# The chunked recurrence of a two-block transformer step: TensorE's twelve steps written as a loop, with one copy of two operands

## The chip, the cores and the metric

The kernel runs on one core of a Trainium2 chip, in float32 with some matmuls in the rounded form fp32r. The metric is the device time of one execution in microseconds (us). Before the change three runs gave 2889.7, 2894.3 and 2896.8 us; the median is 2894.3 us. The profile is of one further execution, whose span is 2891.0 us.

## The reference

The program computes two transformer blocks over 512 latent tokens (the second with 256 context tokens as well). Nearly all of it is left alone by the change. What matters here is one part of the second block, a gated delta rule (RWKV-7), run forward and backward over 768 tokens for 8 heads of 64 dimensions:

```python
def wkv7_scan(state0, r, w, k, v, a_vec, b_vec, reverse):
    xs = tuple(t.transpose(1, 0, 2, 3) for t in (r, w, k, v, a_vec, b_vec))

    def step(S, inp):
        r_t, w_t, k_t, v_t, a_t, b_t = inp
        sa = jnp.einsum('bhij,bhj->bhi', S, a_t)
        S = (S * w_t[:, :, None, :] + sa[..., None] * b_t[:, :, None, :]
             + v_t[..., None] * k_t[:, :, None, :])
        return S, jnp.einsum('bhij,bhj->bhi', S, r_t)

    s_fin, ys = lax.scan(step, state0, xs, reverse=reverse)
    return s_fin, ys.transpose(1, 0, 2, 3)
```

The other parts (projections, two attention mixers, a dense and two sparse feed-forward layers) stand before and after it.

## The kernel before

Each part of the network is a `Stage` with one method for each engine. Semaphores that only count upwards order the engines; `at(name, n, i)` gives the count that item i of step n has when it is done. The stage that changes is `Wkv`, from 1351 to 1672 us of the span. It works through the 768 tokens in `STEPS` = 12 chunks of 64 tokens, with all 8 heads and both directions at once, so that each product is 16 matmuls of 64x64 blocks in the four quadrants of the array.

In a step, VectorE makes two operands from the decays: `removal` (L2362, the factor a that reads the old state before it is replaced) and `reading` (L2367, the factor r that reads the output). They lie in `w.at` and `w.rt`, two copies of each, taken in turn by `n % 2`, so that step n+1's can be made while step n's are in use. The keys are in `w.kt` and `w.bt`. TensorE's step (`step`, from L2158) then does, in this order:

- three turns of 128x128 blocks (`turn`, L2155): tokens to rows; the third waits for `y_added`, since its bank held the last step's output;
- the products of factors ("grams", L2140) of the keys kt with a and with r, and of bt with r;
- five levels of a triangular inverse by doubling: a half product (`half`, L2167), a copy by ScalarE (L2330), then `grow` (L2180) and `grow_turned` (L2188), whose sums VectorE adds (L2425, L2428);
- between the levels, products with the old state (`w_from_state` L2206, `y_from_state` L2214) and with the keys (L2230);
- the next step's first grams (a with bt, both ways), the solution u (L2272), the turned gram (L2149), output and state sums (L2222, L2282, L2286, L2290).

VectorE's step masks the grams (L2377), adds the level sums, makes the next step's removal and reading after levels 1 and 2, then masks the next step's first grams (`low`: L2377 and L2384), makes new keys (L2359), `up` (L2390), adds the state (L2396), the two outputs (L2409), and decays the state (L2402). ScalarE copies and takes exponentials, GpSimd makes kt, bt and the level blocks (L2508).

On TensorE the 12 steps are a Python loop, so the program holds 12 copies of a step's instructions. An earlier stage of the same program, `Experts` (L616, matmuls on L642), is already a loop in the program (`Fori`) on TensorE, ScalarE and VectorE: 288 matmuls a turn, 5 turns, from about 447 to 790 us.

The functions that the diff touches, as they are before:

Of the kernel before, what the change touches and what calls it, by code (L numbers as in the profile page):

```python
# [2028 lines left out]
class Wkv(Stage):  # L2029
# [7 lines left out]
    def __init__(self, k, w, y, ksum):  # L2037
        super().__init__(k)
        self.w, self.y, self.ksum = w, y, ksum
        self.steps = {}  # L2040
        sums = 2 * self.LEVELS - 1
        for name, per in (("exps", 1), ("keyed", 1), ("keys_scaled", 1), ("new_keys", 1), ("factors", 1), ("more_factors", 1),
                          ("key_totals", 1), ("grams", 3), ("tokens", 3), ("token_rows", 3), ("more_grams", 1), ("last_grams", 1),
                          ("presets", 2), ("masked", 3), ("more_masked", 2), ("level_blocks", self.LEVELS),
                          ("level_half", self.LEVELS), ("level_half_copied", self.LEVELS), ("level_summed", sums),
                          ("level_added", sums), ("w_summed", 4), ("w_copied", 1), ("u_summed", 1), ("u_copied", 1),
                          ("state_summed", 1), ("outputs", 1), ("state", 2), ("y_added", 1)):
            self.steps[name] = (*self.count("keys_weighed" if name == "keys_scaled" else "wkv_" + name, per * self.STEPS), per)

# [50 lines left out]
    GRAMS = ((4, 0), (4, 256), (2, 0), (2, 256), (0, 0))  # L2100
    TURNED_GRAM = (2, 0)

# [16 lines left out]
    def tensor(self, pe):  # L2119
# [10 lines left out]
        def operands(n):  # L2130
            at, rt = w.at[n % 2], w.rt[n % 2]
            return (w.bt, at), (at, w.bt), (w.kt, at), (w.bt, rt), (w.kt, rt)

        def gram(n, i):
            lhs, rhs = operands(n)[i]
            first, off = self.GRAMS[i]
            for c in range(4):
                for e, d in corners:
                    at = off + c // 2 * P + self.home(c, d) * 64
                    last = t.matmul(psum[64 * d:64 * d + 64, first + e, at:at + 64], self.by_dim(lhs, c, d, e),  # L2140
                                    self.by_dim(rhs, c, d, e), start=True, stop=True)
            return last

        def turned_gram(n):
            first, off = self.TURNED_GRAM
            for c in range(4):
                for e, d in corners:
                    r, at = 64 * self.home(c, d), off + c // 2 * P + d * 64
                    last = t.matmul(psum[r:r + 64, first + e, at:at + 64], self.by_dim(w.bt, c, d, e),  # L2149
                                    self.by_dim(w.at[n % 2], c, d, e), start=True, stop=True)  # L2150
            return last
# [6 lines left out]
        def step(n):  # L2158
            def half(lv):
                if lv:  # L2160
                    pe.wait_ge(*self.at("level_added", n, self.sum_of(lv - 1, 0)))
                else:
                    pe.wait_ge(*self.at("masked", n, 1))
                    pe.wait_ge(*self.at("token_rows", n, 1))
                pe.wait_ge(*self.at("level_blocks", n, lv))
                for c, e, d in units:
                    last = t.matmul(bank_of(6, d, c, e, self.home(c, d)), self.plain(w.lo[lv % 2], c, e, d), self.plain(w.x, c, e, d),  # L2167
                                    start=True, stop=True)
                last.then_inc(self.sem("level_half"), 1)

            def ready(lv):
                pe.wait_ge(*self.at("level_half_copied", n, lv))
                if lv:
                    pe.wait_ge(*self.at("level_added", n, self.sum_of(lv - 1, 1)))
                elif n:
                    pe.wait_ge(*self.at("state", n - 1, 0))
# [7 lines left out]
            def grow_turned(lv):  # L2184
                if lv == 0:
                    pe.wait_ge(*self.at("more_masked", n, 0))
# [15 lines left out]
            def w_from_state():  # L2202
                pe.wait_ge(*self.at("more_masked", n, 1))
                for c in range(4):
                    for e, d in corners:
                        last = t.matmul(w_of(c, e, d), self.by_dim(w.at[n % 2], c, d, e), self.by_dim(w.s, c, d, e), start=(c == 0),  # L2206
                                        stop=False)
                last.then_inc(self.sem("w_summed"), 1)

            def y_from_state():  # L2210
                pe.wait_ge(*self.at("w_copied", n))
                for c in range(4):
                    for e, d in corners:
                        last = t.matmul(y_of(c, e, d), self.by_dim(w.s, c, d, e), self.by_dim(w.rt[n % 2], c, d, e), start=(c == 0),  # L2214
                                        stop=False)
                last.then_inc(self.sem("w_summed"), 1)

            def y_from_keys():
                pe.wait_ge(*self.at("w_summed", n, 3))
                for c in range(4):  # L2220
                    for e, d in corners:
                        t.matmul(y_of(c, e, d), self.token_rows(w.vr, c, e, d), self.plain(w.rkt, c, e, d), start=False, stop=False)  # L2222

            def w_from_keys(odd):

                pe.wait_ge(*self.at("w_summed", n, odd))
# [7 lines left out]
            def first_grams(m):  # L2234
                pe.wait_ge(*self.at("factors", m))
                gram(m, 0).then_inc(self.sem("grams"), 1)
                gram(m, 1).then_inc(self.sem("grams"), 1)

            if n == 0:
                first_grams(0)  # L2240
                turned_gram(0).then_inc(self.sem("grams"), 1)
            pe.wait_ge(*self.at("more_factors", n))
            turn(6, w.vc)
            turn(7, w.bt)
            if n:
                pe.wait_ge(*self.at("y_added", n - 1))
            turn(0, w.kt)
            pe.wait_ge(*self.at("masked", n, 2))
            gram(n, 2)
            gram(n, 3).then_inc(self.sem("more_grams"), 1)  # L2250
            for lv in range(self.LEVELS):
                half(lv)
                if lv == 0:
                    pe.wait_ge(*self.at("token_rows", n, 2))
                    gram(n, 4).then_inc(self.sem("last_grams"), 1)
# [12 lines left out]
            if n + 1 < self.STEPS:  # L2268
                first_grams(n + 1)
            pe.wait_ge(*self.at("level_added", n, self.sum_of(last_lv, 1)))  # L2270
# [4 lines left out]
            if n + 1 < self.STEPS:  # L2275
                turned_gram(n + 1).then_inc(self.sem("grams"), 1)
            y_from_keys()
            if n + 1 < self.STEPS:
                pe.wait_ge(*self.at("masked", n + 1, 1))
# [3 lines left out]
            pe.wait_ge(*self.at("u_copied", n))  # L2283
# [9 lines left out]
        for n in range(self.STEPS):  # L2293
            step(n)
# [54 lines left out]
    def vector(self, dve):  # L2349
# [12 lines left out]
        def removal(n, d):  # L2362
            e = w.e[:, n % 2].rearrange("p (c d) t -> p c d t", d=2)
            v.scalar_tensor_tensor(out=self.quads(w.at[n % 2])[:, :, d, :], in0=self.nat(w.kk, n, d), scalar=-1.0,
                                   in1=e[:, :, d, 0:CHUNK], op0=ALU.mult, op1=ALU.mult)

        def reading(n, d):  # L2367
            e = w.e[:, n % 2].rearrange("p (c d) t -> p c d t", d=2)
            v.tensor_tensor(out=self.quads(w.rt[n % 2])[:, :, d, :], in0=self.nat(w.r, n, d), in1=e[:, :, d, 1:CHUNK + 1], op=ALU.mult)
# [43 lines left out]
        def step(n):  # L2413
            more = n + 1 < self.STEPS
            dve.wait_ge(*self.at("more_grams", n))
            mask(2, w.lkt, w.strict)
            mask(3, w.rbt, w.incl)
            dve.drain().then_inc(self.sem("more_masked"), 1)
            for lv in range(self.LEVELS):
                if lv == 0:  # L2420
                    dve.wait_ge(*self.at("last_grams", n))
                    mask(4, w.rkt, w.incl).then_inc(self.sem("more_masked"), 1)
# [22 lines left out]
        for d in (0, 1):  # L2445
            removal(0, d)
            reading(0, d)
        replacement(0)
# [6 lines left out]
    def gpsimd(self, pool):  # L2455
        g_, w = self.nc.gpsimd, self.w

        def keyed(n):
            if n:
                pool.wait_ge(*self.at("more_grams", n - 1))  # L2460
# [21 lines left out]
        def more_factors(n):  # L2482
            if n:
                pool.wait_ge(*self.at("last_grams", n - 1))
# [945 lines left out]
class Kernel:  # L3430
# [158 lines left out]
    def block_two(self):  # L3589
# [109 lines left out]
        w.at, w.rt = (self.rstd[:, 0, :], self.rstd[:, 1, :]), (self.rstd[:, 2, :], self.rstd[:, 3, :])  # L3699
# [57 lines left out]
    def moe(self, segs, gain, shift, gate, layer):  # L3757
# [21 lines left out]
          "pv_summed", "head_out")  # L3779
# [348 lines left out]
```

## Time and profile before

| | |
|---|---|
| three runs | 2889.7, 2894.3, 2896.8 us |
| span of the profiled execution | 2891.0 us (its own device time isn't listed apart) |
| TensorE busy, matmuls and weight loads | 2514.2 us (87%), 1944.6 us (67%) |
| VectorE, ScalarE, GpSimd busy | 1647.4 us (57%), 1217.1 us (42%), 426.0 us (15%) |
| stage `Wkv` | 1351 to 1672 us, 12 steps |

### The profile page before, as it was taken

What the parts mean: (1) busy time and instruction counts of PE and PEld (TensorE: products, weight loads), DVE (VectorE), ACT (ScalarE), POOL (GpSimd) and SP (SyncE); (2) the same over time, 40 slices, a digit from 0 to 9 for tenths busy, and PEclk for the clock granted to TensorE, in tenths of its full rate; (3) what the DMA queues carried; (4) which work ended last, traced back from release to release, by engine and by line L of the source; (5) the groups of instructions that cost most, each with busy time, mean ns of one, the idle gap of its engine ahead of it and who ended that gap; (6) DMA issues with size and microseconds to landing.
All of it is one profiled execution on the core that took longest, in us unless ns stands there. A gap on an engine that the chain in (4) does not pass through costs nothing.

```text
span 2891.0 us, 55856 instructions
## 1 busy us (share of the span) xinstructions
PE 2514.2 (87%) x23648; PEld 1944.6 (67%) x23648; DVE 1647.4 (57%) x2360; ACT 1217.1 (42%) x1740; POOL 426.0 (15%) x412
## 2 busy tenths in 40 slices
PE   6979889999978789997877788899987889988996
PEld 5745567787866447785777756777866656767774
DVE  3655545544442374435665563588975365548896
ACT  2423333222232226325333223277864247446784
POOL 1010000000010020003544401123220030012321
PEclk9979989999999779999999988999997989999998
DMA  4247822222221000200000031199963200027995
GB/s 174 88 153 286 330 83 88 91 98 87 87 75 39 15 1 1 92 1 5 5 4 5 5 146 50 66 353 375 347 258 146 80 1 1 16 79 266 357 343 207
DMA packets 63962, 354.48 MB, mean 123 GB/s; under 512 B 15329, under 2 KB 15345, under 8 KB 27248
## 3 DMA queue, kind: packets, MB, share of 16 engines
q1 hardware_dynamic: 41792, 292.60, 26.9%
q0 software_dynamic: 21936, 58.50, 5.5%
q8 instruction: 180, 2.95, 0.4%
q14 instruction: 54, 0.44, 0.0%
HBM read 344.91 MB, written 36.70 MB: 132 GB/s over the span
## 4 chain that ended last, share of the span: by engine, by line
PE 72%; DVE 8%; ACT 5%; issue 5%; DMA 3%; PEld 3%; DVEq 3%; POOL 1%; ACTq 1%; PEldq 0%; POOLq 0%
PE psum L642 13%; PE psum L436 12%; PE psum L3223 9%; PE psum L1187 4%; PE psum L3245 4%; PE psum L1206 3%; PE psum L1827 3%; PE psum L1197 3%; PE psum L2834 2%; PEld psum L436 2%; PE psum L2188 2%; DMA weight_slots<-in_weights 2%; PE psum L1733 2%; PE psum L2167 1%; PE psum L418 1%
## 5 line engine op out<-in xcount | busy, mean ns | idle before, releaser
L436 PE MATMUL psum<-arena_r 128*128 128x512 f32 (+1 forms) x976 | 312.2, 361 | 4.3 <-DVE weight_slots_r L462 4.2
L642 PE MATMUL psum<-arena_r 128*128 128x512 f32 x704 | 250.7, 397 | 10.8 <-issue 3.9
L436 PE MATMUL psum<-arena_r,weight_slots_r 128*128 128x512 f32 (+1 forms) x696 | 248.9, 358 | 0.0
L457 ACT ACTIVATE arena_r<-weight_slots 128x1024 fp32r<-128x1024 f32 x73 | 76.4, 1057 | 338.4 <-PE psum L436 251.0
L642 PE MATMUL psum<-arena_r,weight_slots_r 128*128 128x512 f32 x528 | 209.1, 396 | 0.0
L436 PEld LDWEIGHTS psum<-arena_r 128*128 128x128 f32 x976 | 179.1, 190 | 36.1 <-issue 4.3
L436 PE MATMUL psum<-h_t_r,arena_r 128*128 128x512 f32 (+1 forms) x528 | 192.6, 365 | 0.0
L3177 DVE TENSOR_TENSOR weight_slots_r<-weight_slots,arena_r 128x2048 fp32r<-128x2048 f32 x78 | 177.7, 2289 | 21.5 <-ACT arena_r L3172 20.9
L3177 DVE TENSOR_TENSOR weight_slots_r<-weight_slots,h_t_r 128x2048 fp32r<-128x2048 f32 x72 | 164.0, 2290 | 20.4 <-ACT h_t_r L3172 19.7
L642 PEld LDWEIGHTS psum<-arena_r 128*128 128x128 f32 x704 | 133.8, 190 | 45.5 <-issue 13.5
L1271 DVE TENSOR_REDUCE stat<-psum 128x1 f32<-128x768 f32 (+1 forms) x112 | 98.7, 882 | 108.9 <-PE psum L1187 108.7
L3223 PE MATMUL psum<-weight_slots_r,arena_r 128*128 128x512 f32 x400 | 157.7, 394 | 0.0
L3172 ACT ACTIVATE arena_r<-weight_slots 128x2048 fp32r<-128x2048 f32 x78 | 148.4, 1920 | 19.1 <-DMA weight_slots<-in_weights 18.4
L436 PEld LDWEIGHTS psum<-arena_r,weight_slots_r 128*128 128x128 f32 x696 | 131.6, 189 | 20.4
L3172 ACT ACTIVATE h_t_r<-weight_slots 128x2048 fp32r<-128x2048 f32 x72 | 137.0, 1921 | 18.5 <-DMA weight_slots<-in_weights 18.0
L3223 PE MATMUL psum<-arena_r 128*128 128x512 f32 x416 | 132.0, 398 | 9.9 <-issue 8.1
L642 PE MATMUL psum<-h_t_r,arena_r 128*128 128x512 f32 x352 | 140.3, 399 | 0.0
L1187 PE MATMUL psum<-arena 64*128 64x384 f32 (+2 forms) x416 | 122.3, 536 | 8.6 <-POOL arena L1237 4.9
L3223 PE MATMUL psum<-h_t_r,arena_r 128*128 128x512 f32 x384 | 122.4, 400 | 5.7 <-issue 4.6
L642 PEld LDWEIGHTS psum<-arena_r,weight_slots_r 128*128 128x128 f32 x528 | 100.2, 190 | 22.6
L462 DVE TENSOR_TENSOR weight_slots_r<-weight_slots,arena_r 128x1024 fp32r<-128x1024 f32 x73 | 88.3, 1219 | 45.2 <-ACT arena_r L457 44.3
L3331 POOL DMA_INDIRECT arena<-h_rows,arena x50 | 72.9, 1457 | 274.6 <-PE psum L3188 190.4
(466 smaller groups left out, 5516.5 us busy)
## 6 DMA issues: line engine op xcount, KB each, us to landing
weight_slots<-in_weights SPq DMA_DIRECT2D x277, 1024.0 KB, 6.8
arena<-y_rows POOLq DMA_DIRECT2D x20, 512.0 KB, 7.8
h_rows<-arena POOLq DMA_DIRECT2D x10, 512.0 KB, 3.0
x_keep<-x_t POOLq DMA_DIRECT2D x1, 3072.0 KB, 9.0
x_t<-x_keep POOLq DMA_DIRECT2D x2, 1536.0 KB, 9.1
x_t<-in_x POOLq DMA_DIRECT2D x1, 2048.0 KB, 9.7
out_x<-x_t SPq DMA_DIRECT2D x1, 2048.0 KB, 7.2
arena<-in_toe POOLq DMA_DIRECT2D x1, 1792.0 KB, 7.6
```

Of the source, the lines that this page charges most:

```text
L436: last = self.nc.tensor.matmul(self.bank(n), w[:, kt, :], self.operand(part, kt, a, b), start=(i == 0), stop=(i == len(passes) - 1))
L462: self.nc.vector.tensor_tensor(out=self.tile_weights(self.kern.slots_r, t), in0=self.tile_weights(self.kern.slots, t), in1=self.w_hi[:, t ...
L642: last = nc.tensor.matmul(bank, w(p, k), x(q, k), start=(k == j == 0), stop=(k == n - 1 and j == 2))
L1187: last = t_.matmul(s[:, r, a:b], q, key[:, a:b], start=True, stop=True)
L1197: last = t_.transpose(self.turned_bank(u)[:, i * P:(i + 1) * P], self.probs[:, u % 2, i * P:(i + 1) * P], kern.ident)
L1206: last = t_.matmul(self.out_bank()[64 * e:64 * e + 64, :], self.units[u][2](i), self.probs_t[:, u % 4, i * P:(i + 1) * P], start=(i == 0), ...
L1271: v.reduce_max(kern.row_max[:, par], self.score_bank(u), mybir.AxisListType.XY)
L1827: last = self.nc.tensor.matmul(self.bank(n), w, x, start=(i == 0), stop=(i == len(pairs) - 1))
L3172: self.nc.scalar.activation(self.weights(item)[0], x, ACT.Copy).then_inc(self.rounded[0], 1)
L3177: self.nc.vector.tensor_tensor(out=self.kern.slots_r[:, slot, :], in0=self.kern.slots[:, slot, :], in1=hi.bitcast(F32), op=ALU.subtract).t ...
L3223: last = nc.tensor.matmul(ps[t % 2], x[:, t % 2, kt * P:(kt + 1) * P], w[:, k, :], start=(kt == 0 and i == 0), stop=(kt == KT - 1 and i == 2))
L3245: last = nc.tensor.matmul(ps[5 + half], x[:, t % 2, k * P:(k + 1) * P], w[:, k, half * 512:(half + 1) * 512], start=(k == 0 and i == 0), s ...
```

## The change

TensorE's steps 0 to 10 become one body in a `Fori` loop, and step 11 stands behind it. Since a loop's body has fixed addresses, the two copies of a and r become one, `w.ar`, in which each head's and direction's 64 columns of a stand beside its 64 columns of r. The grams of kt with a and of kt with r are then one product with 128 moving columns (`key_grams`). Each wait in the loop compares against a register (`due`), which is raised behind the wait. VectorE may write a only when `w_from_state` has read it (`w_summed`, item 0) and r only when `y_from_state` has (item 3), so both readings move behind the last level. A new semaphore `read` tells TensorE that r is there. Two GpSimd waits change places with the grams. The masks of kt with a and with r now come first, and that of bt with r third.

```diff
+    TURNS = {"factors": (1,), "more_factors": (0,), "y_added": (-1,), "masked": (2, 4), "read": (0,), "token_rows": (1, 2),
+             "level_blocks": tuple(range(5)), "level_half_copied": tuple(range(5)), "level_added": tuple(range(9)),
+             "state": (-2,), "more_masked": (0, 1), "w_summed": (0, 1, 3), "w_copied": (0,), "u_copied": (0,)}
...
+        def key_grams():
+            for c in range(4):
+                for e, d in corners:
+                    at = c // 2 * 256 + self.home(c, d) * P
+                    last = t.matmul(psum[64 * d:64 * d + 64, 2 + e, at:at + P], self.by_dim(w.kt, c, d, e),
+                                    self.both(w.ar, c, d, e), start=True, stop=True)
+            return last
...
+        def wait(name, n, i=0):
+
+            if isinstance(n, int):
+                pe.wait_ge(*self.at(name, n, i))
+                return
+            turns = self.TURNS[name]
+            k, per = turns.index(i), self.steps[name][2]
+            following = turns[k + 1] if k + 1 < len(turns) else turns[0] + per
+            pe.wait_ge(self.sem(name), due[name])
+            pe.reg_add(due[name], due[name], following - i)
...
-            pe.wait_ge(*self.at("masked", n, 2))
-            gram(n, 2)
-            gram(n, 3).then_inc(self.sem("more_grams"), 1)
+            wait("masked", n, 2)
+            wait("read", n)
+            key_grams().then_inc(self.sem("more_grams"), 1)
...
-        for n in range(self.STEPS):
-            step(n)
+        due = {}
+        for name, turns in self.TURNS.items():
+            due[name] = pe.alloc_register("wkv_due_" + name)
+            pe.reg_mov(due[name], self.at(name, 0, turns[0])[1])
+        first_grams(0, 0)
+        turned_gram().then_inc(self.sem("grams"), 1)
+        pe.wait_ge(*self.at("masked", 0, 1))
+        with pe.Fori(0, self.STEPS - 1) as n:
+            step(n, True)
+        step(self.STEPS - 1, False)
...
             dve.wait_ge(*self.at("more_grams", n))
-            mask(2, w.lkt, w.strict)
-            mask(3, w.rbt, w.incl)
+            for i, (dst, m) in enumerate(((w.lkt, w.strict), (w.rkt, w.incl))):
+                v.tensor_tensor(out=self.four(dst), in0=self.key_grams(i), in1=spread(m), op=ALU.mult)
...
                     if lv == 1:
                         dve.wait_ge(*self.at("exps", n + 1))
+                        dve.wait_ge(*self.at("w_summed", n, 0))
                     removal(n + 1, lv - 1)
-                    reading(n + 1, lv - 1)
...
             if more:
+                dve.wait_ge(*self.at("w_summed", n, 3))
+                reading(n + 1, 0)
+                reading(n + 1, 1)
+                dve.drain().then_inc(self.sem("read"), 1)
                 low(n + 1)
...
-                pool.wait_ge(*self.at("more_grams", n - 1))
+                pool.wait_ge(*self.at("last_grams", n - 1))
...
-                pool.wait_ge(*self.at("last_grams", n - 1))
+                pool.wait_ge(*self.at("more_grams", n - 1))
...
-        w.at, w.rt = (self.rstd[:, 0, :], self.rstd[:, 1, :]), (self.rstd[:, 2, :], self.rstd[:, 3, :])
+        w.ar = self.rstd[:, 0:2, :].rearrange("p a b -> p (a b)")
```

The program's order shows it at two places. First TensorE, at the end of a step and the start of the next, up to level 0. Before (L2286 and L2290 are the state's and the output's last sums, L2155 the turns, L2140 the grams):

```order
L2286 MATMUL psum<-x_t,arena 64x64 x15
L2290 MATMUL psum<-arena,x_t 64x64 x16
L2155 MATMUL psum<-consts,arena 128x128 [waits wkv_more_factors]
L2155 MATMUL psum<-consts,arena 128x128 x7
L2155 MATMUL psum<-consts,arena 128x128 [waits wkv_y_added]
L2155 MATMUL psum<-consts,arena 128x128 x3
L2140 MATMUL psum<-rstd,arena 64x64 [waits wkv_masked]
L2140 MATMUL psum<-rstd,arena 64x64 x31
L2167 MATMUL psum<-arena 64x64 [waits wkv_level_blocks,wkv_token_rows,wkv_masked]
```

In the changed program the body begins so (L2184 the turns, L2169 the key grams, L2211 the half product, L2201 the helper `wait`):

```order
L2201 REGISTER_ALU [waits wkv_more_factors]
L2184 MATMUL psum<-consts,arena 128x128 x8
L2201 REGISTER_ALU [waits wkv_y_added]
L2184 MATMUL psum<-consts,arena 128x128 x4
L2201 REGISTER_ALU [waits wkv_masked]
L2201 REGISTER_ALU [waits wkv_read]
L2169 MATMUL psum<-rstd,arena 64x128 x16
L2201 REGISTER_ALU [waits wkv_token_rows]
L2201 REGISTER_ALU [waits wkv_level_blocks]
L2211 MATMUL psum<-arena 64x64 x16
```

and it ends so, with the turn back (L2321 and L2325 are the last sums):

```order
L2201 REGISTER_ALU [waits wkv_u_copied]
L2321 MATMUL psum<-x_t,arena 64x64 x16
L2325 MATMUL psum<-arena,x_t 64x64 x16
L2335 REGISTER_ALU
L2335 COMPARE_AND_BRANCH
```

Thirty-two grams became sixteen with twice the columns; a step has 444 matmuls of the program instead of 460; and 36 register steps, most with a wait, and a branch came in. Second VectorE, from the last level to the state. Before:

```order
L2428 TENSOR_TENSOR arena<-arena,psum 128x512 [waits wkv_level_summed]
L2377 TENSOR_TENSOR arena<-psum,x_t 128x512 [waits wkv_grams]
L2384 COPY_PREDICATED arena<-x_t,psum 128x512 [waits wkv_presets]
L2359 TENSOR_TENSOR arena<-arena 128x4x64 [waits keys_weighed]
L2359 TENSOR_TENSOR arena<-arena 128x4x64
L2390 COPY_PREDICATED arena<-x_t,psum 128x512 [waits wkv_presets,wkv_grams]
L2396 TENSOR_TENSOR arena<-arena,psum 128x512 [waits wkv_state_summed]
```

In the changed program (L2471 is the level's sum, L2412 the readings, L2420 and L2427 `low`, L2439 the state):

```order
L2471 TENSOR_TENSOR arena<-arena,psum 128x512 [waits wkv_level_summed]
L2412 TENSOR_TENSOR rstd<-arena 128x4x64 [waits wkv_w_summed]
L2412 TENSOR_TENSOR rstd<-arena 128x4x64
L2420 TENSOR_TENSOR arena<-psum,x_t 128x512 [waits wkv_grams]
L2427 COPY_PREDICATED arena<-x_t,psum 128x512 [waits wkv_presets]
L2402 TENSOR_TENSOR arena<-arena 128x4x64 [waits keys_weighed]
L2402 TENSOR_TENSOR arena<-arena 128x4x64
L2433 COPY_PREDICATED arena<-x_t,psum 128x512 [waits wkv_presets,wkv_grams]
L2439 TENSOR_TENSOR arena<-arena,psum 128x512 [waits wkv_state_summed]
```

The two readings left the levels and stand between the last level's sum and `low`.

## Rows read from the trace of the kernel before

**Rows 1.** The page: span, busy time, and the queue with TensorE's instructions.
```profile
span 2891.0 us, 55856 instructions
PE 2514.2 (87%) x23648; PEld 1944.6 (67%) x23648; DVE 1647.4 (57%) x2360; ACT 1217.1 (42%) x1740; POOL 426.0 (15%) x412
...
q8 instruction: 180, 2.95, 0.4%
```

**Rows 2.** Busy time and instructions by stretch, ten steps of the recurrence.
```profile
core 0: us, PE busy (x) PEld busy (x) DVE busy (x) ACT busy (x) POOL busy (x), PEclk, DMA share, GB/s
1380.00:1646.00 266.00, 212.44 (x9103) 192.99 (x9095) 160.52 (x262) 83.50 (x160) 130.78 (x141) 0.99 0.02 5
```

**Rows 3.** TensorE's waits in that stretch: us in total, times, longest.
```profile
PE psum L2180 <- ACT arena L2330: 8.9, 35, 0.3
PE psum L2188 <- issue: 6.8, 11, 1.0
...
PE psum L2155 <- DVEq L2411: 1.6, 7, 0.2
...
PE psum L2206 <- issue: 0.8, 1, 0.8
PE psum L2167 <- DVE arena L2425: 0.6, 2, 0.3
```

**Rows 4.** DMA queues in the same stretch: packets, MB.
```profile
q8 instruction: 72, 1.18, 1.9%
```

**Rows 5.** DMA from 1362 to 1382 us, in 40 slices of 0.5 us.
```profile
GB/s 0 33 0 0 0 0 0 0 33 0 0 0 0 0 0 0 33 0 0 0 0 0 0 33 0 0 0 0 0 0 33 0 0 0 0 0 0 33 0 0
DMA packets 6, 0.10 MB, mean 5 GB/s; under 512 B 0, under 2 KB 0, under 8 KB 0
q8 instruction: 6, 0.10, 2.0%
```

**Rows 6.** The chain of waits through one step: start, us, what.
```profile
1382.20 1.09 PE psum L2140 x64
...
1384.43 0.04 issue
...
1385.17 0.92 PE psum L2188 x32
...
1403.31 1.37 issue
1404.67 0.52 PE psum L2286 x20
...
1405.30 0.69 DVE arena L2396
...
1406.32 0.08 issue
...
1406.96 0.66 PE psum L2155 x4
```

**Rows 7.** DMA from 1401 to 1405 us, in 40 slices of 0.1 us.
```profile
GB/s 0 0 0 0 0 0 0 82 0 0 0 0 164 0 0 0 0 0 0 0 0 0 0 0 0 0 0 0 0 0 0 0 0 0 0 0 0 0 0 0
```

**Rows 8.** `Experts`, four turns of its loop: busy time by stretch, then DMA queues.
```profile
506.00:779.00 273.00, 269.59 (x1163) 217.87 (x1161) 134.22 (x163) 71.05 (x63) 0.00 (x0) 1.00 0.25 92
q1 hardware_dynamic: 3456, 25.17, 24.8%
q14 instruction: 1, 0.01, 0.0%
```

**Rows 9.** VectorE in order of time at a step's end: start, us, what, idle before.
```profile
1399.55 0.69 DVE L2428 TENSOR_TENSOR arena<-arena,psum 128x512 f32<-128x512 f32 x1 [1.74 <-PE psum L2188]
1400.57 0.69 DVE L2377 TENSOR_TENSOR arena<-psum,x_t 128x512 f32<-128x512 f32 x1 [0.33 <-PE psum L2140]
...
1403.16 0.73 DVE L2390 COPY_PREDICATED arena<-x_t,psum 128x512 f32<-128x512 int32 x1 [0.19 <-issue]
```

**Rows 10.** VectorE in the ten steps by line: the readings.
```profile
L2369 DVE TENSOR_TENSOR rstd<-arena 128x256 f32<-128x256 f32 x20 | 12.7, 633 | 0.0
```

More of the change, by code:

```diff
@@ L2139, in gram, with turned_gram @@
                     at = off + c // 2 * P + self.home(c, d) * 64
[L2140 to L2144 removed]
+                    last = t.matmul(psum[64 * d:64 * d + 64, first + e, at:at + 64], lhs(left, c, d, e), rhs(right, c, d, e),
+                                    start=True, stop=True)
+            return last
+        def key_grams():
[5 more added lines that the diff above has]
+            return last
+        def turned_gram():
             first, off = self.TURNED_GRAM
@@ L2156, in turn, with first_grams, step @@
             last.then_inc(self.sem("tokens"), 1)
-        def step(n):
+        def first_grams(n, ahead):
+            wait("factors", n, ahead)
+            gram(0).then_inc(self.sem("grams"), 1)
+            gram(1).then_inc(self.sem("grams"), 1)
+        def wait(name, n, i=0):
[7 more added lines that the diff above has]
+            pe.reg_add(due[name], due[name], following - i)
+        def step(n, more):
             def half(lv):
                 if lv:
-                    pe.wait_ge(*self.at("level_added", n, self.sum_of(lv - 1, 0)))
+                    wait("level_added", n, self.sum_of(lv - 1, 0))
                 else:
-                    pe.wait_ge(*self.at("masked", n, 1))
-                    pe.wait_ge(*self.at("token_rows", n, 1))
-                pe.wait_ge(*self.at("level_blocks", n, lv))
+                    wait("token_rows", n, 1)
+                wait("level_blocks", n, lv)
                 for c, e, d in units:
@@ L2171, in ready @@
             def ready(lv):
-                pe.wait_ge(*self.at("level_half_copied", n, lv))
+                wait("level_half_copied", n, lv)
                 if lv:
-                    pe.wait_ge(*self.at("level_added", n, self.sum_of(lv - 1, 1)))
-                elif n:
-                    pe.wait_ge(*self.at("state", n - 1, 0))
+                    wait("level_added", n, self.sum_of(lv - 1, 1))
+                else:
+                    wait("state", n, -2)
             def grow(lv):
@@ L2202, in w_from_state @@
             def w_from_state():
-                pe.wait_ge(*self.at("more_masked", n, 1))
+                wait("more_masked", n, 1)
                 for c in range(4):
                     for e, d in corners:
-                        last = t.matmul(w_of(c, e, d), self.by_dim(w.at[n % 2], c, d, e), self.by_dim(w.s, c, d, e), start=(c == 0),
+                        last = t.matmul(w_of(c, e, d), self.removing(w.ar, c, d, e), self.by_dim(w.s, c, d, e), start=(c == 0),
                                         stop=False)
@@ L2210, in y_from_state @@
             def y_from_state():
-                pe.wait_ge(*self.at("w_copied", n))
+                wait("w_copied", n)
                 for c in range(4):
                     for e, d in corners:
-                        last = t.matmul(y_of(c, e, d), self.by_dim(w.s, c, d, e), self.by_dim(w.rt[n % 2], c, d, e), start=(c == 0),
+                        last = t.matmul(y_of(c, e, d), self.by_dim(w.s, c, d, e), self.reading(w.ar, c, d, e), start=(c == 0),
                                         stop=False)
@@ L2218, in y_from_keys @@
             def y_from_keys():
-                pe.wait_ge(*self.at("w_summed", n, 3))
+                wait("w_summed", n, 3)
                 for c in range(4):
@@ L2224, in w_from_keys @@
             def w_from_keys(odd):
-                pe.wait_ge(*self.at("w_summed", n, odd))
+                wait("w_summed", n, odd)
                 for e in (0, 1):
@@ L2267, in step @@
                 grow_turned(lv)
-            if n + 1 < self.STEPS:
-                first_grams(n + 1)
-            pe.wait_ge(*self.at("level_added", n, self.sum_of(last_lv, 1)))
+            if more:
+                first_grams(n, 1)
+            wait("level_added", n, self.sum_of(last_lv, 1))
             for c, e, d in units:
@@ L2274, in step @@
             last.then_inc(self.sem("u_summed"), 1)
-            if n + 1 < self.STEPS:
-                turned_gram(n + 1).then_inc(self.sem("grams"), 1)
+            if more:
+                turned_gram().then_inc(self.sem("grams"), 1)
             y_from_keys()
-            if n + 1 < self.STEPS:
-                pe.wait_ge(*self.at("masked", n + 1, 1))
+            if more:
+                wait("masked", n, 4)
             for c in range(4):
@@ L2447, in vector @@
             reading(0, d)
+        dve.drain().then_inc(self.sem("read"), 1)
         replacement(0)
```

57 lines of the change are left out of this document (31 added, 26 removed).

## The prediction

> **What bounds the kernel now.** I read four views, in this order. The page says that TensorE is busy for 87% of the span, and that queue q8 brought it 180 packets of instructions, 2.95 MB, so 16 KB each [rows 1]. It doesn't say where that matters. The busy time by stretch then gives the recurrence: in 266 us TensorE did 9103 matmul and 9095 load instructions, which at 908 of each in a step (448 float32 matmuls as two, and 12 turns) is ten steps of 26.5 us, while VectorE was busy for 160.5 us, 60% [rows 2]. The waits say what TensorE stood idle for: besides 0.3 us at a time for ScalarE's copies, fourteen lines end in "issue", from 6.8 us before L2188 to 0.8 us before L2206, 41.7 us together [rows 3]. "Issue" means that no semaphore held it. That is 4.2 us a step, and the reader should ask what it is, since nearly all of this change's worth is there.
>
> The DMA view answers it. In the same stretch q8 moved 72 packets, 7.2 a step [rows 4]; (9103 + 9095) / 72 = 253 matmul and load instructions a packet, and with the waits about 256. In 20 us six packets stand in the 2nd, 9th, 17th, 24th, 31st and 38th half-microsecond: one every 3.5 to 3.6 us, never two close together [rows 5]. Laid over the chain: TensorE runs out at 1403.31 and goes on at 1404.67 [rows 6], and the packet before that came in the slice from 1402.2 us, about 1 us earlier than TensorE stops and 2.4 us before it goes on [rows 7]. I read this as one packet in flight at a time, asked for when TensorE enters the one before, some 3.5 us from the asking to the use. So 7.2 packets x 3.5 to 3.6 us is 25 to 26 us: the step is bound by the delivery of its own instructions, and the dependencies lie just under it.
>
> The Trainium skill ("Runtime: NRT & Kernel Launch", "Instruction fetch mechanics") calls this delivery hidden behind the sequencer's own pace. By that rule the 41.7 us would be something else and the loop would save none of it; the rows just named speak against it here, at 3.5 us a packet.
>
> **Does a loop keep its instructions?** `Experts` shows it. Four turns of 288 matmuls ran from 506 to 779 us, 1163 matmuls and 1161 loads, 9 packets' worth, and q8 isn't among that stretch's queues [rows 8]. A turn is 576 such instructions and some waits, 2.4 packets, so at least three packets stay and the way back finds them. The new body is longer: 444 matmuls of the program, 432 of them in two passes, are 876 matmul and 876 load instructions; with 36 register steps and the branch 1789, which is 6.99 packets. Unless it starts within three instructions of a packet's edge it lies across 8, and on entering the eighth TensorE asks for a ninth. No row shows whether eight stay. Both ends of this unknown are large: all stay (saving below), or none (first rival).
>
> **The change part by part**, for one turn of the loop when all stays, against 26.5 us:
>
> - The 4.2 us of "issue" go [rows 3]. What is late next is the dependency chain, PE and VectorE in turn.
> - Key grams: before 64 passes in 1.09 us on the chain [rows 6]. Now 32 passes with twice the columns. Bounds: half, 0.55, if a pass is a matter of issue, and 1.09 if of columns. L2188, 32 passes, took 0.92 us there, and I take that: 0.2 less.
> - VectorE's readings: twenty took 12.7 us, 0.63 each [rows 10]. In the levels they stood beside TensorE, so taking them out gives nothing. At the end they stand in front of `low`. The last level's sum starts at 1399.55, `low` at 1400.57 after 0.33 us of waiting for grams, and `up` ends at 1403.89 [rows 9]. Two readings and their drain take between 0.75 us, if they overlap as neighbours do, and 1.3 us; 0.33 us of it falls into the wait. `up` then ends 0.4 to 1.0 us later. Queued behind it are the state, the outputs and, through `y_added`, the third turn of the next step. Today VectorE sits idle there until L2396 at 1405.30 [rows 6], because TensorE is late by its packet. With that cover gone VectorE's queue becomes the later one: TensorE would be ready for the state about 0.6 us before `up` ends. I charge 1.0 us; bounds 0 and 1.9.
> - The wait on `read` costs nothing: it is raised before `low`, on whose result the wait in front of it (`masked`) hangs anyway. The wait on `w_summed` item 0 stands after level 1, whose second product TensorE does after `w_from_state`: already there.
> - GpSimd: the two exchanged waits are for grams that TensorE finishes at level 0, far ahead of its need; kt follows the new keys, which VectorE now makes 0.4 to 1.0 us later, still ahead of `y_added`. Nothing.
> - The 36 register steps: where TensorE has work queued they cost nothing. On the chain they are paid after each copy by ScalarE (two of them, five levels) and at some four other places. No row shows one; a handover costs 0.04 us, and 0.08 us behind a drain [rows 6]. Bounds 0 and 36 x 0.08 = 2.9 us; I take 14 at 0.08, 1.1 us.
> - The branch: in `Experts` TensorE was busy for 269.6 of 273 us through four of them [rows 8], so at most 0.8 us each; it meets the step's start, where TensorE waits for VectorE. I take 0.1.
>
> Sum: -4.2 - 0.2 + 1.0 + 1.1 + 0.1 = -2.2 us. The first pass through the body is fetched as today, so ten turns gain: -22 us. The first pass and the last step, still bound by packets, save 64 instructions each, a quarter of a packet, 0.9 us each, and the first pays the register steps: together about -1. The span goes from 2891.0 to 2868; the runs' median stands 3.3 us above the profiled span, so 2871 us. The first bounds of each term together give at best -4.7 (key grams by half, 0 elsewhere), 2847; at worst, still with all resident, +1.4 a turn or 2908.
>
> **The rivals.**
>
> *The body doesn't stay, and every packet comes again* (slower). The mechanism is the replacement of the oldest packet: with room for no more than eight, the ninth displaces the first, whose return displaces the second, and so on. For it: the body is three times the one that is known to stay. Against it: nothing in the trace but that a loop of three packets does. Price: nine packets at 3.5 us are 31.5 us a turn, 5.0 more than 26.5, and the way back has no packet underway: +50 us, 2944. It decides as soon as eight packets and one don't fit.
>
> The Trainium skill (same page and section) gives TensorE 128 KiB of instruction memory, 2048 instructions, and in the same place says that only two blocks are kept and that a branch out of them waits for a fetch. `Experts` contradicts the two. The 2048 would hold 1789 but not nine blocks: by this figure the change would be slower.
>
> *One packet is lost a turn* (about the same, or slower). If places are fixed, the ninth takes only the first's. The turn back then waits for one packet. Asked for at once, it is there 3.5 us after the branch; the chain from L2396 to the third turn covers 1.7 us of that (1405.30 to 1406.96), and the first eight turns of blocks, 1.1 us, come after: about 2 us more than the 24.3 of the sum, 26.3, so 2892. Asked for behind the ninth, 5.5 us more: 29.8, so 2927. I take the middle, 2910.
>
> *The stalls are the crossing, not the packet*: TensorE pauses at each 256th instruction even when the next is there. Then 4.2 us stay and 2.0 come: +20 us, 2914. `Experts` can't tell, since its matmuls are long enough to cover a pause. Against it: the fixed distance from packet to restart.
>
> *The change does more than I charge*: the tail and register steps hide, up to the 2847 above.
>
> **How the numbers follow.** All stays 0.46, with 2871 and a range of its own from 2850 to 2890; one packet lost 0.24; all lost 0.21; crossing 0.05; better than 2855 0.04. The first is the likeliest, so 2871. The range reaches up into the second rival's slower half: 2853 to 2930 leaves out the first rival (0.21) and little else. Within 0.3% (8.7 us, about what a measurement of this kernel can tell from no change) lies half of the second rival: 0.12. Faster 0.48, from the first case nearly whole and the last; slower 0.40.
>
> **What would show it.** Right: from the loop's second turn to its end no q8 packet, about 108 packets on the page instead of 180, no "issue" gaps above 0.2 us, turns of 24.3 us, and VectorE's L2439 following L2433 without a wait. The first rival: packets every 3.5 us through the loop, as before, nine a turn. The second: two packets a turn, at its end, and one gap of 3.5 to 7 us before the turns of blocks, with the rest free of gaps. The third: no packets but gaps. The readings: if `low` starts less than 0.7 us after the last level's sum ends, my charge for the tail is wrong. If the handover from ScalarE's copy (L2330 before) to `grow` takes more than 0.3 us, the register steps are dearer than taken. The forecast as a whole is wrong if the ninth packet displaces the first.

## The result

Nine runs of the changed kernel gave a median of 2909.6 us (2900.9 to 2915.5), against 2894.3 us (2884.4 to 2904.1) of the kernel before: a ratio of 1.0057, 95% interval 1.0041 to 1.0074. It is slower by 15 us, where 23 us faster was forecast. The forecast is wrong, and its range of 2853 to 2930 us holds the time only because it reached into the rivals.

The page of the changed kernel shows fewer packets and a longer span, which answers to [rows 1]:

```profile
span 2903.6 us, 55426 instructions
PE 2518.7 (87%) x23264; PEld 1951.6 (67%) x23264; DVE 1639.2 (56%) x2360; ACT 1216.9 (42%) x1740; POOL 426.3 (15%) x412
...
q8 instruction: 153, 2.51, 0.4%
```

That is 27 packets fewer than before, not the 72 that a body that always stays would save. The loss lies in the recurrence: from the first turn to the start of the last step 306.5 us pass (1358.5 to 1665.0), and before it was 291.2 (1354.3 to 1645.5), 15 us less. What stands ahead of the recurrence and behind it differs by some us from one execution to the next, so the runs below are compared by their turns as well.

The turns of the loop are not alike. By the starts of their turns of blocks (L2184), turns 0 to 10 take 28.9, 28.1, 28.6, 27.4, 26.7, 27.5, 28.4, 27.4, 28.6, 27.5 and 27.5 us, and the q8 packets that come in them number 6, 2, 7, 2, 7, 2, 7, 2, 7, 2 and 7. Turns 1 and 2, in 40 DMA slices of 1.45 us from 1387 to 1445 us:

```profile
GB/s 0 0 0 0 0 0 0 0 0 0 0 0 0 0 6 0 28 0 0 0 11 0 0 11 0 0 0 11 0 11 0 0 11 0 11 0 0 11 0 0
...
q8 instruction: 9, 0.15, 1.3%
```

There is no TensorE packet for 23 us (the 6 is another engine's), then come two together and a third, and then one every 3.6 to 5.6 us. Close up, 1409 to 1417 us in slices of 0.2 us:

```profile
GB/s 0 0 0 0 0 0 0 0 0 123 0 0 82 0 0 0 0 0 0 0 0 0 0 0 0 0 0 0 0 0 0 0 0 0 0 82 0 0 0 0
```

One packet starts at 1410.9 (with another engine's in its slice), one at 1411.6, and the next at 1416.1. The chain of waits through the same place says what they cost:

```profile
1407.79 0.32 DVE arena L2420
1408.11 1.81 issue
1409.92 1.28 POOL arena L2535
1411.20 0.06 POOLq L2536
1411.26 4.26 issue
1415.52 2.79 PE psum L2184 x12
1418.31 1.92 PE psum L2169 x32
1420.23 0.81 PE psum L2211 x32
```

TensorE stands for 4.3 us after everything that it waits for is done. What it does in that time stands in the trace as well. The turn back itself (L2335) has a record, and in turn 1 it lasts from 1410.5 to 1415.4. From 1391 to 1634 us:

```profile
L2335 PEldq COMPARE_BRANCH  x9: 212/4491/4834, 1410.5 to 1632.8; - x9
```

The three figures are the shortest, the median and the longest in ns: five turns back took 4.5 to 4.8 us, and four took 0.2. The five are those with two packets. And what follows is slow: twelve turns of blocks in 2.79 us and the key grams in 1.92. The busy time by stretch says why, in the column of the granted clock:

```profile
1387.50:1410.80 23.30, 20.35 (x877) 18.82 (x876) 14.81 (x26) 8.33 (x16) 10.01 (x13) 1.00 0.00 0
1410.80:1415.50 4.70, 0.07 (x7) 0.01 (x1) 2.13 (x4) 0.00 (x0) 4.38 (x5) 0.83 0.06 9
1415.50:1421.00 5.50, 5.48 (x90) 5.17 (x94) 0.70 (x2) 1.79 (x3) 0.36 (x1) 0.52 0.01 3
1421.00:1444.10 23.10, 18.07 (x800) 16.45 (x792) 12.82 (x22) 6.64 (x13) 10.54 (x12) 1.00 0.02 4
```

The clock was 1.00 (2.4 GHz) through turn 1, in which the body was resident (no packet came). It fell in the 4.7 us in which TensorE did nothing, and stood at 0.52, so nearly all at 1.2 GHz, for the 5.5 us behind. So turn 1 did its work in 23.3 us without a packet, 3.2 us less than a step before [rows 2], and gave it back twice: 4.7 us of standing, and some 2 us of slow clock in the turn behind it, which then fetched seven packets as well. Behind the other four stands the half product (L2211) began 3.7 to 4.5 us after the turn's start; in turns 1, 3, 5, 7 and 9, which have no stand ahead, it was 2.7.

### The profile page after: what moved, and what is told of

Its sections match the earlier page's. It is cut to its first block, busy times and chain, and to the rows that moved or that the text cites. A ratio compares the mean times of both kernels' runs of the same rounds, so it can differ in the third digit from the quotient of the medians.

```text
span 2903.6 us, 55426 instructions
## 1 busy us (share of the span) xinstructions
PE 2518.7 (87%) x23264; PEld 1951.6 (67%) x23264; DVE 1639.2 (56%) x2360; ACT 1216.9 (42%) x1740; POOL 426.3 (15%) x412
## 4 chain that ended last, share of the span: by engine, by line
PE 71%; DVE 7%; ACT 5%; issue 5%; DMA 3%; PEld 3%; DVEq 3%; POOL 1%; ACTq 1%; PEldq 0%; POOLq 0%; SPq 0%
PE psum L642 13%; PE psum L436 12%; PE psum L3271 9%; PE psum L1187 4%; PE psum L3293 3%; PE psum L1206 3%; PE psum L1827 3%; PE psum L1197 3%; PE psum L2882 2%; PEld psum L436 2%; DMA weight_slots<-in_weights 2%; PE psum L2232 2%; PE psum L1733 2%; PE psum L2211 1%; PE psum L418 1%
## 5 line engine op out<-in xcount | busy, mean ns | idle before, releaser
L642 PE MATMUL psum<-arena_r 128*128 128x512 f32 x704 | 251.0, 397 | 10.8 <-issue 3.9
```

What stands on the lines that cost most here:

```text
L642: last = nc.tensor.matmul(bank, w(p, k), x(q, k), start=(k == j == 0), stop=(k == n - 1 and j == 2))
```

## The experiments

**Is it the packets?** Theory, formed on this trace: eight packets have room. The body lies across eight; on entering the eighth TensorE asks for the ninth, and this displaces the first, which is missing at the turn back. Its return displaces the second, and so on through the next turn. Three placements of the same body test it. Identity matmuls in front of the loop, behind which TensorE waits for the first factors, move its start within a packet from 57 instructions to 1, to 157 and to 13; they write a bank that is rewritten later, and the whole computation is done. (The 57 is a count of the program; the trace bears it out. At the end of turn 0 of the changed kernel TensorE stands for its last packet and then does 26 of L2325's 32 passes. With their loads and the two instructions of the turn back these are 54, as the count gives for the eighth packet.)

```
+        for _ in range(50):          # 25 and 53 in the other two
+            t.matmul(psum[0:64, 6, 0:64], ident[0:64, 0:64], ident[0:64, 0:64], start=True, stop=True)
         first_grams(0, 0)
```

> The changed kernel with 50 idle 64x64 float32 matmuls of the identity (200 instructions) before the recurrence's first grams, where TensorE waits for factors anyway. They move the loop's body from 57 instructions into a 16 KB packet to 1, so that it lies in seven packets and the one asked for behind it is the eighth. Theory: eight packets have room, and the ninth displaces the first in every second turn. Then no q8 packet comes from turn 1 to turn 10, no gap of 4.5 us stands at a turn's start, turns take 23.5 to 24.5 us and the time is 2865 to 2880 us. Rival: the 4.5 us at a turn's start are a wait for GpSimd's late kt and the branch; then turns stay at 27.5 to 28 and the time at 2905 to 2912 us.

Measured 2866.4 us, ratio to the kernel before 0.9906 (0.9891 to 0.9922). From 1391 to 1623 us, ten turns, the DMA queues hold no q8 at all:

```profile
DMA packets 6, 0.05 MB, mean 0 GB/s; under 512 B 0, under 2 KB 0, under 8 KB 0
## 3 DMA queue, kind: packets, MB, share of 16 engines
q14 instruction: 6, 0.05, 0.1%
```

and a turn takes 23.25 us (turns 2 to 9, alike to 0.02 us), a little under the 23.5 expected. TensorE's waits from 1391 to 1623 us are these alone:

```profile
PE psum L2224 <- ACT arena L2375: 16.8, 40, 0.4
PE psum L2317 <- DVE arena L2429: 5.9, 10, 0.9
PE psum L2184 <- POOLq L2538: 4.6, 9, 0.5
PE psum L2184 <- DVEq L2456: 0.2, 1, 0.2
```

No line ends in "issue", though a turn still crosses six edges between packets: the pause at each crossing, the prediction's third rival, is ruled out. The turn back took 0.21 us in each of turns 1 to 9. The same instructions, 56 places earlier in a packet, are worth 43 us.

The identity matmuls aren't free, though:

```profile
1349.14 10.79 PE L2333 MATMUL psum<-consts 64*64 64x64 f32 x99 [4.06 <-issue]
1359.62 0.38 PE L2161 MATMUL psum<-rstd,arena 64*64 64x64 f32 x3
```

In the changed kernel TensorE waits for 8.1 us there. Here the first grams (L2161) start 15.7 us after L1961's last group starts, there 9.2. So the 43 us are what is left after some 6 us of cost; a start in the right place without them would gain about 6 us more, which is an estimate.

> The changed kernel with 25 such idle matmuls (100 instructions): the body starts 157 instructions into a packet and has 154 instead of 54 in its eighth. Theory, with the oldest packet displaced: TensorE is in the eighth packet long enough in every turn for the ninth to be asked for, so every turn misses its first packet and, one after the other, the rest: nine packets a turn, 29 to 31 us a turn, 2925 to 2945 us. If packets had fixed places: one lost a turn, two packets a turn, 27 to 28 us, 2900 to 2910 us. Rival (late kt and branch): no change from the changed kernel, 2905 to 2912 us.

Measured 2961.7 us, ratio 1.0243 (1.0228 to 1.0259), slower even than expected. One turn, 1486 to 1519 us, in slices of 0.8 us:

```profile
GB/s 20 0 0 0 0 20 0 0 0 0 20 0 0 0 0 20 0 0 0 0 0 20 0 0 0 20 0 0 0 20 0 0 0 0 20 20 0 0 10 0
...
q8 instruction: 9, 0.15, 2.1%
```

Nine packets, two of them together at the turn back, and 33 us a turn. Fixed places would have given two packets a turn: this is ruled out. The expectation of 29 to 31 us left out the low clock behind each stand: the granted clock of that turn is 0.91. It also took 3.5 us a packet, where nine in 33 us are 3.7. How the missing 2 us divide wasn't tried.

> As the run with 50 idle matmuls, with 53 (212 instructions): the body starts 13 instructions into a packet, so it lies across eight, with 10 instructions in the last, and the one behind is the ninth. Theory: the ninth is fetched only if TensorE is still in the eighth packet some tenths of a microsecond after entering it; ten instructions are too few, so no packet comes from turn 1 on and the time is that of 50 idle matmuls, 2864 to 2870 us. Rival: entering the eighth is enough; then the first packet is displaced in most turns, with gaps of 4.5 us and 2900 us or above.

Measured 2918.4 us, ratio 1.0093 (1.0075 to 1.0111): the theory's addition falls. It also shows that idle matmuls as such are not what helped: three more of them than in the first run cost 52 us. Ten instructions in the eighth packet can be enough. But not always: turns 1, 6, 7 and 10 of the profiled run had no packet, turns 2, 4 and 8 ended with the pair, and each of those was followed by one with seven. (Turn 7 took 23.2 us. The other three took 24.7 to 25.2; each follows a turn that fetched, and over its first 5 us the granted clock was 0.66. Turn 7 follows one that fetched nothing, and there it was 1.00.) So entering the eighth starts a request that a quick turn back sometimes forestalls. In the changed kernel, with 54 instructions there, it was forestalled in turns 0, 2, 4, 6 and 8, where TensorE came to the eighth packet straight from a stand for it (in turn 0 from 1386.85, with the turn back done by 1387.3). It was not in turns 1, 3, 5, 7 and 9, where TensorE came to it in the run of its work. That reading is argued from the times of those ten turns, and it doesn't cover the run with 53, where both outcomes came in the run of the work. What exactly decides wasn't tried.

**Is it the length too?** The key grams as two sets of 64 columns again, same start:

```
+            for off, part in ((0, self.removing), (64, self.reading)):
...
-                    last = t.matmul(psum[64 * d:64 * d + 64, 2 + e, at:at + P], self.by_dim(w.kt, c, d, e),
+                        last = t.matmul(psum[64 * d:64 * d + 64, 2 + e, at:at + 64], self.by_dim(w.kt, c, d, e),
...
```

> As the run with 50 idle matmuls, but the key grams are two sets of 64 columns again, written to the same places: 64 instructions more, a body of 1853 that starts 1 instruction into a packet and has 62 in its eighth. Theory: with the ninth packet asked for, the turns miss and cascade again by turns, 27 to 29 us, 2900 to 2920 us, though the same start kept 1789 instructions resident at 2866 us. Rival: the start is what matters and not the length; then 0.1 us a turn more than 50 idle matmuls, 2868 us.

Measured 2915.2 us, ratio 1.0057 (1.0041 to 1.0073), and from turn 1 on packets 2, 7, 2, 7 by turns: the changed kernel's picture, with a body that starts well but is 64 instructions too long. Merging the key grams is what lets the body fit seven packets; without the start it is worth little.

**What is the rest of the change worth?** The same kernel with its loop written out:

```
-        with pe.Fori(0, self.STEPS - 1) as n:
+        for n in range(self.STEPS - 1):
             step(n, True)
```

> The changed kernel with its loop written out again (a Python loop with constant waits): one copy of a and r, the merged key grams and the late readings stay, the loop and the register steps go. Theory: the step is bound by packets, 6.95 instead of 7.2, so 25.3 to 26.3 us a step and 2884 to 2892 us; the loss of the changed kernel is then all the loop's. Rival: the one copy's late readings on VectorE are what costs; then steps take 27 us or more and the time is 2900 us or above.

Measured 2887.0 us, ratio 0.9985 (0.9973 to 0.9996): 26.0 us a step over 11 steps (1352.8 to 1638.5), a packet every 3.8 us in the mean. One copy, late readings and merged grams together cost nothing there; if anything there is a small gain, at 0.15% hardly beyond the noise. The changed kernel's loss is the loop's.

**What binds once the packets are gone?** With 50 identity matmuls, the readings before the last level's turned sum instead of behind it:

```
+                if lv == self.LEVELS - 1 and more:
+                    dve.wait_ge(*self.at("w_summed", n, 3))
+                    reading(n + 1, 0)
+                    reading(n + 1, 1)
+                    dve.drain().then_inc(self.sem("read"), 1)
                 dve.wait_ge(*self.at("level_summed", n, self.sum_of(lv, 1)))
```

> As the run with 50 idle matmuls, and VectorE makes the two readings before it adds the last level's turned sum, once y_from_state has read the old ones, instead of behind it. Theory: with no packets to wait for, VectorE's tail is on the chain, and this takes 0.6 to 0.9 us off each turn: 6 to 9 us less than the run with 50 idle matmuls. Rival: something else is late there (GpSimd's kt, the third turn), and it is the same within 2 us.

Measured 2857.9 us, ratio 0.9885 (0.9872 to 0.9899). That is 8.5 us less than the first run, as expected, but a turn, at 22.76 us, is only 0.5 us shorter and not 0.6 to 0.9; the turns account for 5 us. TensorE's remaining wait at a turn's start is for GpSimd's kt, 0.5 us. So VectorE's new keys were also moved after level 3, and kt between GpSimd's presets:

```
                 if lv == 3 and more:
                     replacement(n + 1)
+                    new_keys(n + 1)
...
                 preset_plain(n + 1)
-                preset_turned(n + 1)
                 more_factors(n + 1)
+                preset_turned(n + 1)
```

> As the run with 50 idle matmuls and early readings, and VectorE makes the next step's new keys after level 3 instead of behind the masks, and GpSimd makes kt between its two presets instead of behind both. Theory: in the resident loop the chain at a turn's end runs over the masks, the new keys, GpSimd's 1.3 us for kt and then the turns; with kt early the eight turns of blocks that don't need y_added run beside VectorE, 0.8 to 1.6 us less a turn, 2842 to 2850 us. Rival: y_added was as late as kt, so at most 0.3 us a turn, 2855 us.

Measured 2872.8 us, ratio 0.9927 (0.9913 to 0.9941): 15 us worse than without, and both theories missed. The turn grew to 24.03 us. VectorE in order of time at its end:

```profile
1481.40 0.97 DVE L2404 TENSOR_TENSOR arena<-arena 128x256 f32<-128x256 f32 x2
1482.49 1.84 DVE L2414 TENSOR_TENSOR rstd<-arena 128x256 f32<-128x256 f32 x2
1484.45 0.69 DVE L2478 TENSOR_TENSOR arena<-arena,psum 128x512 f32<-128x512 f32 x1
```

and GpSimd at the same time:

```profile
1482.54 1.51 POOL L2538 TENSOR_TENSOR arena<-arena 128x512 f32<-128x512 f32 x1 [0.78 <-issue]
```

The two readings, 0.76 us in the run before, took 1.84 us: the second started at 1482.83 and ended at 1484.33, after GpSimd's kt had (1484.05). The new keys, 0.97 us, stood in front of them. So the last level's sum (L2478), on which TensorE waits, started 1.7 us after its product ended, where it was 0.06. That kt is what slowed the readings is read from the overlap; the last run, without it, agrees. Exchanging TensorE's two waits before a level's second product,

```
-                wait("level_half_copied", n, lv)
                 if lv:
                     wait("level_added", n, self.sum_of(lv - 1, 1))
                 else:
                     wait("state", n, -2)
+                wait("level_half_copied", n, lv)
```

> As the run with early new keys, and TensorE waits for the level's turned sum (long there) before it waits for ScalarE's copy, so that one register step instead of two stands between the copy and the next product. Theory: the 0.22 us from the copy to the product, against 0.04 us in the kernel before, are the two register steps; one fewer gives 0.09 us at four handovers a turn, 3 to 4 us in all. Rival: the 0.22 us are the queue refilling behind a wait; no change.

Measured 2869.1 us, ratio 0.9919 (0.9904 to 0.9934), and 23.70 us a turn, 0.33 less: the pause between ScalarE's copy and the product went from 0.22 to 0.12 us. The intervals of the two times overlap, so it is the turns that show this. A register step is worth some 0.1 us where it stands behind a wait on the chain.

The version with early keys was also run with its loop written out, with constant waits and without identity matmuls:

> The same early readings and new keys without the loop, without register steps and without idle matmuls. Theory: the written-out steps are bound by their packets, so a shorter chain gives nothing: 2884 to 2890 us, as the unrolled run with late readings (2887). Rival: the chain counts there too; then it gives 1 us a step or more, 2875 us or less.

Measured 2890.1 us (ratio 0.9982, 0.9969 to 0.9994), 26.3 us a step. It doesn't tell much of a shorter chain, as the new order was itself slower; but its ratio can't be told from the 0.9985 of the other unrolled run, so most of this loss, 0.8 us a turn in the resident loop, is hidden where packets bind.

Last, the version that these point to: 50 identity matmuls, early readings and exchanged waits as above, new keys after level 2, where VectorE has over a microsecond to itself, and kt before both presets.

```
+                if lv == 2 and more:
+                    new_keys(n + 1)
...
+                more_factors(n + 1)
                 preset_plain(n + 1)
                 preset_turned(n + 1)
-                more_factors(n + 1)
```

> As the run with early new keys and the exchanged waits, but VectorE makes the new keys after level 2, where it has 1.3 us to itself, and GpSimd makes kt before both presets, so that neither meets the two readings at the last level. Theory: the turn of 24.0 us with early new keys was VectorE's last-level queue (new keys, and readings slowed beside GpSimd's kt), so moving it gives 21.8 to 22.4 us a turn and 2845 to 2853 us, below the 2858 of early readings alone. Rival: what the early readings gained is all there is; 2855 us or more.

Measured 2856.6 us, ratio 0.9851 (0.9831 to 0.9871), the fastest against its own comparison; the kernel with early readings alone had 0.9885. The turn, 22.22 us, came out as the theory said. The time didn't: it lies above the 2845 to 2853 us expected, where the rival had put it. But the kernel before took 2900.0 us in that session and 2892.6 in the one of the early readings, so the two times can't be compared straight; by the turns it is 0.54 us a turn better. How much of that is the exchanged waits and how much the order wasn't taken apart. A level of a turn:

```profile
1441.69 0.61 ACT arena L2375
1442.30 0.12 issue
1442.42 0.69 PE psum L2224 x32
1443.12 0.92 PE psum L2232 x32
1444.04 0.06 issue
1444.09 0.73 PE psum L2211 x32
```

and at the turn's end VectorE's readings take 0.76 us again, in a stretch in which it waits for TensorE anyway:

```profile
1450.99 0.68 DVE L2418 TENSOR_TENSOR arena<-arena 128x512 f32<-128x512 f32 x1
1452.04 0.76 DVE L2414 TENSOR_TENSOR rstd<-arena 128x256 f32<-128x256 f32 x2 [0.36 <-PE psum L2258]
1453.07 0.69 DVE L2478 TENSOR_TENSOR arena<-arena,psum 128x512 f32<-128x512 f32 x1 [0.27 <-PE psum L2232]
```

## Why the prediction was wrong, step by step

**What bounds the kernel: right.** The steps wait for their own instructions. Written out, they stay at 26 us with two different chains; resident, the same work takes 23.25 us. One reading was a little off: 3.5 to 3.6 us a packet came from 20 us of the trace, and 72 packets in 266 us [rows 2, rows 4] are 3.7 each, which gives the 26.5 us step fully.

**Does a loop keep its instructions: this step failed.** It counted the body rightly as 6.99 packets lying across eight, and named the ninth. Then it took "all stay" as the likeliest, 0.46, though the only row for it was a loop of three packets [rows 8]. The runs show room for eight and not for nine: seven and the next stay, eight and the next don't. The prediction's own last sign came true: the ninth packet displaces the first. The Trainium skill ("Runtime: NRT & Kernel Launch", "Instruction fetch mechanics") gives TensorE 2048 instructions, which is eight packets of 256: the runs agree, and it was the rule that spoke against the change. That only two blocks are kept, which the same section says, the runs contradict: with 50 identity matmuls ten turns of seven packets each passed without a fetch.

**The rivals.** The mechanism of the first, the oldest packet replaced and the rest in turn, is the true one, but only every second turn. The prediction had it in every turn or in none, since it took the request for the ninth as certain. That mixture puts 2910 us between its 2944 and the 2871; that the second rival's middle says 2910 is chance, since fixed places are ruled out. The third, a pause at each crossing, is ruled out by the waits of the resident loop. The fourth, more gain than charged, didn't come either: even resident, this change took 2866.4 us and not 2847. The first two left out the clock. Behind a stand of 4.7 us it was down, and work at 0.52 behind it cost about 2 us: twelve turns of blocks and the key grams took 4.71 us where the resident loop takes 2.57 (1.54 and 1.03).

**The terms of the sum**, read in the loop that does stay. The sum gave 24.3 us; it is 23.25.
- The 4.2 us of "issue" went whole: right.
- Key grams: 0.92 us taken, 1.03 measured, so 0.06 us gained and not 0.2.
- The readings: 1.0 us charged; moving them away gives 0.5. The prediction's sign for this, `low` less than 0.7 us after the last level's sum, did not catch it: it was 0.86 (1433.37 to 1434.23).
- GpSimd: "nothing" was wrong. With 50 identity matmuls the chain at a turn's end runs over it:

```profile
1434.23 0.67 DVE arena L2422
1434.89 1.43 issue
1436.32 1.38 POOLq L2538
1437.70 0.12 issue
1437.82 1.54 PE psum L2184 x12
```

TensorE starts the turn only when kt is done, since all twelve turns of blocks stand behind its one wait. It stands idle for 0.5 us a turn there.
- Register steps: 1.1 us taken. A copy's handover takes 0.22 us instead of 0.04, so 0.18 for two; with four such on the chain, 0.7 us.

Of the single terms none that a run sizes was off by more than 0.5 us. Put together, the measured ones give 23.5 us, and 24.0 with GpSimd's wait, against 23.25: they overlap, and no run takes them apart further. The sum was off by 1.0 us a turn, some 10 us in ten turns; the placement by 43.

## What to carry to other kernels

Where an engine is idle with no semaphore to blame, count its instruction packets against the time; here one every 3.7 us was a bound of its own. In these runs the loop paid when its body's packets and the one behind them stayed together, so count packets from the real start of the body, not from its length. If the count is one too many, a few dummy instructions ahead of the loop may be worth more than the whole rewrite, but measure what they cost: here 50 matmuls took 10.8 us where 8.1 were free. And a stand on TensorE, 4.7 us here, can be paid again in its clock.

## What the runs showed of the hardware that was not expected

- TensorE kept eight packets, of about 256 instructions. With a ninth asked for in every turn, they went oldest first, so a loop that is one packet too long fetched nine a turn (33 us) and not one.
- The request for the next packet is not certain. With 10 or 54 instructions before the turn back it came in some turns and not in others, which made turns of one kernel differ by packets of 0, 2 and 7.
- Two requests can be close together: the ninth and the first came 0.1 to 1.1 us apart, while packets fetched in line never came closer than 3.2 us. TensorE's stand was 4.0 to 4.8 us and not 7.
- VectorE's 128x256 operations without PSUM took 0.76 us for two where GpSimd did no arithmetic beside them, and 1.84 us beside one GpSimd operation of 1.51 us.
